# The delta rule's triangular inverse in 32x32 blocks, turned on VectorE

## What is computed

```python
decay = jnp.exp(jnp.where(causal, gc[..., :, None] - gc[..., None, :], -jnp.inf))
kb = k * beta[..., None]
lower = jnp.where(strict, jnp.einsum('nhcid,nhcjd->nhcij', kb, k) * decay, 0.0)
rhs = jnp.concatenate([v * beta[..., None], kb * jnp.exp(gc)[..., None]], axis=-1)
uw = lax.linalg.triangular_solve(lower, rhs, left_side=True, lower=True, unit_diagonal=True)
...
def step(state, inp):
    u_c, w_c, qk_c, qg_c, kd_c, a_c = inp
    v_new = u_c - jnp.einsum('nhik,nhkv->nhiv', w_c, state)
    o = jnp.einsum('nhik,nhkv->nhiv', qg_c, state) + jnp.einsum('nhij,nhjv->nhiv', qk_c, v_new)
    state = state * a_c[..., None, None] + jnp.einsum('nhjk,nhjv->nhkv', kd_c, v_new)
    return state, o
```

## Time and profile before

| | |
|---|---|
| three executions | 3165.36, 3160.8, 3163.7 us; median 3163.7 |
| the profiled execution | 3158.29 us, span 3156.2 us |
| mean granted clock of TensorE | 0.97 |
| TensorE busy | 2999.3 us, 95% of the span |
| GpSimd, ScalarE, VectorE busy | 1617.3, 1248.1, 1244.8 us |
| the chain that ended last | TensorE 85%, VectorE 5%, GpSimd 4%, ScalarE 3% |

### The profile page before, as it was taken

How to read it: one execution, slowest core, us unless ns; L and a number is a source line. 1 busy time by engine, 2 the same in 40 slices (tenths; PEclk the granted TensorE clock), 3 DMA queues, 4 the chain that set the end, 5 groups by cost and what they waited for, 6 DMA issues and landing times.

```text
span 3156.2 us, 47130 instructions
## 1 busy us (share of the span) xinstructions
PE 2999.3 (95%) x19462; PEld 2584.0 (82%) x19462; DVE 1244.8 (39%) x2298; ACT 1248.1 (40%) x2122; POOL 1617.3 (51%) x810
## 2 busy tenths in 40 slices
PE   8999999989999899999999999899999898998899
PEld 5777878779999777777777888589999698997899
DVE  2222135524444422211322114745335776622570
ACT  3222234335555332222322224454445556544453
POOL 4333443344443443344433445168887276596587
PEclk9999999999999999999999999899999899998999
DMA  6544224310000144432454323435545153354255
GB/s 251 176 167 148 94 94 156 109 47 1 1 1 1 47 168 178 161 107 94 142 178 135 105 92 88 82 115 189 185 155 176 45 169 112 108 168 140 94 188 167
DMA packets 96884, 381.45 MB, mean 121 GB/s; under 512 B 10369, under 2 KB 15649, under 8 KB 87201
## 3 DMA queue, kind: packets, MB, share of 16 engines
q1 hardware_dynamic: 87456, 311.33, 30.5%
q10 hardware_dynamic: 9216, 67.11, 6.2%
HBM read 374.21 MB, written 4.19 MB: 120 GB/s over the span
## 4 chain that ended last, share of the span: by engine, by line
PE 85%; DVE 5%; POOL 4%; ACT 3%; issue 1%; DMA 1%; SPq 0%; ACTq 0%; POOLq 0%; DVEq 0%
PE bank L220 23%; PE bank L221 22%; PE bank L222 22%; PE bank L750 5%; PE bank L293 2%; POOL weights_lo L213 2%; PE bank L1388 1%; DVE norm_work L447 1%; PE bank L769 1%; DVE norm_work L441 1%; DVE square_sums L405 1%; ACT dn_xt L1036 1%; PE bank L375 1%; ACT weights_hi L203 0%; PE bank L847 0%
## 5 line engine op out<-in xcount | busy, mean ns | idle before, releaser
L213 POOL TENSOR_TENSOR weights_lo<-weights_landing,weights_hi 128x1024 fp32r<-128x1024 f32 x554 | 1334.8, 2413 | 1192.7 <-ACT weights_hi L203 1191.7
L203 ACT ACTIVATE weights_hi<-weights_landing 128x1024 fp32r<-128x1024 f32 x554 | 586.5, 1060 | 1319.6 <-PE bank L222 1238.6
L220 PE MATMUL bank<-normed_hi,weights_lo 128*128 128x256 f32 (+1 forms) x2864 | 979.6, 342 | 39.5 <-POOL normed_lo L463 23.3
L221 PE MATMUL bank<-normed_lo,weights_hi 128*128 128x256 f32 (+1 forms) x2864 | 963.5, 336 | 0.0
L222 PE MATMUL bank<-normed_hi,weights_hi 128*128 128x256 f32 (+1 forms) x2864 | 962.3, 336 | 0.0
L220 PEld LDWEIGHTS bank<-normed_hi,weights_lo 128*128 128x128 f32 x2864 | 546.3, 191 | 133.2 <-issue 32.3
L222 PEld LDWEIGHTS bank<-normed_hi,weights_hi 128*128 128x128 f32 x2864 | 545.6, 190 | 61.5
L221 PEld LDWEIGHTS bank<-normed_lo,weights_hi 128*128 128x128 f32 x2864 | 546.5, 191 | 56.3
L221 PE MATMUL bank<-hidden_lo,weights_hi 128*128 128x512 f32 (+1 forms) x960 | 329.3, 343 | 0.0
L222 PE MATMUL bank<-hidden_hi,weights_hi 128*128 128x512 f32 (+1 forms) x960 | 329.3, 343 | 0.0
L220 PE MATMUL bank<-hidden_hi,weights_lo 128*128 128x512 f32 (+1 forms) x960 | 329.3, 343 | 0.0
(11 more groups left out here) (414 smaller groups left out, 3906.0 us busy)
## 6 DMA issues: line engine op xcount, KB each, us to landing
weights_landing<-w_up SPq DMA_DIRECT2D x176, 512.0 KB, 3.5
ada_landing<-w_ada ACTq DMA_DIRECT2D x64, 1024.0 KB, 4.9
weights_landing<-w_down SPq DMA_DIRECT2D x88, 512.0 KB, 3.5
weights_landing<-w_dn SPq DMA_DIRECT2D x33, 512.0 KB, 3.5
weights_landing<-w_mlp_up SPq DMA_DIRECT2D x32, 512.0 KB, 3.5
weights_landing<-w_mlp_down SPq DMA_DIRECT2D x32, 512.0 KB, 3.6
weights_landing<-w_gate SPq DMA_DIRECT2D x24, 512.0 KB, 4.3
weights_landing<-w_xbc SPq DMA_DIRECT2D x24, 512.0 KB, 3.5
```

The costliest lines, as they stand in the source:

```text
L203: k.nc.scalar.activation(k.WH[:, u % SLOTS, :], k.W[:, u % LANDS, :], ACT.Copy).then_inc(*k.AC.mark(("unit hi", u)))
L213: k.nc.gpsimd.tensor_tensor(k.WL[:, u % SLOTS, :], k.W[:, u % LANDS, :], k.WH[:, u % SLOTS, :].bitcast(F32), ALU.subtract).then_inc(*k.PO. ...
L220: nc.tensor.matmul(out, ll, rh, start=start, stop=False, skip_group_check=True)
L221: nc.tensor.matmul(out, lh, rl, start=False, stop=False, skip_group_check=True)
```

## The change

The blocks up to 32 are kept as such. Levels 1 to 4 no longer work on 128x128 matrices but on the four 32x32 diagonal blocks of each chunk, which lie at their own partitions: `yb` and `xb` hold [128, 4 chunks, 32]. `blocks` issues one small matmul for each chunk and block, so 16 for each direction in place of 4. The turned Y is made by VectorE's blockwise transpose (`turned`) in place of TensorE's turns and ScalarE's copies. Level 5 has 32x32 products off the diagonal (two for each chunk), and `dx`, which gives the turned second block directly. Level 6 keeps its 64x64 products, with `xt` and `p6` as operands. `at` has two buffers, so levels 5 and 6 read it unmasked. GpSimd now copies the diagonal blocks of `at` together (`ad`, four copies), makes `ym`, `y0` and four masks of 128 columns each, and later spreads `xb` and `yb` to `xt` and the wide Y (`spread`, two and four copies a direction); the wide Y is zeroed once. GpSimd also takes the product `qg` from VectorE (`queries`), in its order ahead of `spread`. `kv`, `decay` and `kq` of the next head move one slot ahead, to 1, 2 and 4, and with them `tokens`, `growth`, ScalarE's `decay` and `differences`; `products` stays in slot 5. The head's first products no longer wait for turns that stood ahead of the u products of the head before.

```diff
-LEVELS = 7
+BLK, SMALL = 32, 5
+LAST = 6
...
+def pairs(d):
+    return ((0, 1), (2, 3)) if d == 0 else ((1, 0), (3, 2))
+def blocks(k, bank, at, which, lhs, rhs, name):
+    for c in range(CHUNKS):
+        for rows, to in which:
+            mm = k.nc.tensor.matmul(bank[block(to), at + c * BLK:at + (c + 1) * BLK], lhs(rows, to, c), rhs(rows, to, c), start=True, stop=True)
+    mm.then_inc(*k.PE.mark(name))
+EACH = [(b, b) for b in range(P // BLK)]
...
+def head_p_pe(k, pe, i, s, d):
+    p = i % 2
+    pe.wait_ge(*k.DV.after("head", i, "x" if s < LAST else "y", s - 1, d))
+    if s < SMALL:
+        pe.wait_ge(*k.PO.after("head", i, "lm", s, d))
+        if s == 1 and i:
+            pe.wait_ge(*k.DV.after("head", i - 1, "y", LAST, d))
+        blocks(k, k.B[d], 0, EACH, lambda r, q, c: k.lm[d][block(r), s - 1, c, :], lambda r, q, c: k.xb[p][d][block(r), c, :], ("head", i, "p", s, d))
...
+def head_dy_pe(k, pe, i, s, d):
+    p = i % 2
+    pe.wait_ge(*k.AC.after("head", i, "ps", s, d))
+    if s < SMALL:
+        blocks(k, k.B[d], 0, EACH, lambda r, q, c: k.pb[d][block(r), c, :], lambda r, q, c: k.yb[p][d][block(r), c, :], ("head", i, "dy", s, d))
...
+KV_SLOT, DECAY_SLOT, KQ_SLOT = 1, 2, 4
...
+    def masks(i, d):
+        y, ad, p = k.yb[i % 2][d], k.ad[d], i % 2
+        pool.wait_ge(*k.DV.after("head", i, "at", d, 3))
...
+        for b in range(P // BLK):
+            if b:
+                pool.wait_ge(*k.PO.after("head", i, "ad", d, b - 1))
+            nc.gpsimd.tensor_copy(ad[block(b)], k.at_[p][d][block(b), :, block(b)]).then_inc(*k.PO.mark(("head", i, "ad", d, b)))
...
+        nc.gpsimd.tensor_tensor(y[:], ad[:], level_mask(k, d, 0), ALU.mult).then_inc(*k.PO.mark(("head", i, "ym", d)))
+        pool.wait_ge(*k.PO.after("head", i, "ym", d))
+        nc.gpsimd.tensor_tensor(y[:], ident, y[:], ALU.subtract).then_inc(*k.PO.mark(("head", i, "y0", d)))
+        for s in range(1, SMALL):
+            if i:
+                pool.wait_ge(*k.PE.after("head", i - 1, "p", s, d))
+            nc.gpsimd.tensor_tensor(k.lm[d][:, s - 1], ad[:], level_mask(k, d, s), ALU.mult).then_inc(*k.PO.mark(("head", i, "lm", s, d)))
+    def spread(i, d):
...
     for i in range(DN_HEADS):
+        for d in range(2 if i + 1 < DN_HEADS else 0):
+            queries(i + 1, d)
         for d in range(2):
+            spread(i, d)
+        for d in range(2 if i + 1 < DN_HEADS else 0):
+            masks(i + 1, d)
...
+                if s < LAST:
+                    nc.scalar.activation(flat(k.pb[d][:]), B[d][:, 0:P], ACT.Copy).then_inc(*k.AC.mark(("head", i, "ps", s, d)))
...
+    def sums(i, s, d):
+        y, dy = k.yb[i % 2][d], B[d][:, 0:P]
+        dve.wait_ge(*k.PE.after(*(("head", i, "dx", d) if s == SMALL else ("head", i, "dy", s, d))))
+        if s < SMALL:
+            nc.vector.tensor_tensor(flat(y[:]), flat(y[:]), dy, ALU.subtract).then_inc(*k.DV.mark(("head", i, "y", s, d)))
...
+    def turned(i, s, d):
+        if s:
+            dve.wait_ge(*k.DV.after("head", i, "y", s, d))
+        else:
+            dve.wait_ge(*k.PO.after("head", i, "y0", d))
...
+        nc.vector.transpose(flat(k.xb[i % 2][d][:]), flat(k.yb[i % 2][d][:])).then_inc(*k.DV.mark(("head", i, "x", s, d)))
...
             for d in range(2 if levels else 0):
+                sums(i, s, d)
+            for d in range(2 if levels and s < SMALL else 0):
+                turned(i, s, d)
...
             if after and s == 6:
                 queries(i + 1)
+                for d in range(2):
+                    turned(i + 1, 0, d)
```

More of the change, by code:

```diff
@@ L865, in heads_pe @@
     head_kq_pe(k, pe, 0)
-    for d in range(2):
-        head_first_turn_pe(k, pe, 0, d)
     for i in range(DN_HEADS + 1):
         levels, after = i < DN_HEADS, i + 1 < DN_HEADS
-        for s in range(1, LEVELS):
+        for s in range(1, LAST + 1):
             for d in range(2 if levels else 0):
[L872 to L878, removed]
+                head_p_pe(k, pe, i, s, d)
             if s == 1 and i:
@@ L885, in heads_pe @@
             for d in range(2 if levels else 0):
[L886 to L891 removed]
+                head_dy_pe(k, pe, i, s, d)
             if i and s <= CHUNKS:
@@ L896, in heads_pe @@
                 head_stat_pe(k, pe, i - 1)
-            if after and s == 2:
+            if after and s == KV_SLOT:
                 head_kv_pe(k, pe, i + 1)
-            if after and s == 3:
+            if after and s == DECAY_SLOT:
                 head_decay_pe(k, pe, i + 1)
-            if after and s == 5:
+            if after and s == KQ_SLOT:
                 head_kq_pe(k, pe, i + 1)
-            for d in range(2 if levels and s < LEVELS - 1 else 0):
-                pe.wait_ge(*k.DV.after("head", i, "y", s, d))
-                turns(k, k.B[d], lambda c: k.Y[i % 2][d][:, c, :], ("head", i, "yT", s, d))
@@ L1027, in heads_act @@
                 root(3, 4)
-            if after and s == 2:
+            if after and s == KV_SLOT:
                 tokens(i + 1)
+            if after and s in (2, 3):
+                growth(i + 1, s - 2)
             if after and s in (3, 4):
-                growth(i + 1, s - 3)
-            if after and s in (4, 5):
-                decay(i + 1, s - 4)
-            for d in range(2 if levels and s < LEVELS - 1 else 0):
-                act.wait_ge(*k.PE.after("head", i, "yT", s, d))
-                nc.scalar.activation(w4(k.XT[d]), B[d][:], ACT.Copy).then_inc(*k.AC.mark(("head", i, "x", s, d)))
-        for d in range(2 if after else 0):
-            first_x(i + 1, d)
+                decay(i + 1, s - 3)
         for d in range(2 if levels else 0):
@@ L1111, in heads_dve @@
                     ins.then_inc(*k.DV.mark(("head", i - 1, "state", s - 1, d)))
-            if after and s in (3, 4):
-                differences(i + 1, s - 3)
+            if after and s in (2, 3):
+                differences(i + 1, s - 2)
             if after and s == 5:
```

186 lines of the change are left out of this document (109 added, 77 removed).

## The result

| | before | after |
|---|---|---|
| executions | 5 | 5 |
| median, us | 3161.86 (3159.61 to 3165.36) | 3059.42 (3045.72 to 3065.1) |
| the profiled execution, its span | 3158.29, 3156.2 | 3045.72, 3043.9 |
| first u of head 0, last head's u starting at | 719.8, 1024.78 | 705.5, 920.26 |
| a head, us | 43.6 | 30.7 |

In the profiled executions the difference is 112.6 us, where I forecast 65. 104.4 of it lie in this stage. The other 8 lie mostly 900 us later, in the window attention (61.8 us after, 69.1 before), which the change doesn't touch. TensorE's granted clock over that stretch was 0.97 after and 0.90 before.

The account below looks back on a forecast made before the run. TensorE was taken to bound the stage at 43.6 us a head. Slots 9.7 + 4.6 + 4.0 + 5.0 and border 11.8 gave 35.1, saving 59.5 over seven heads plus 6 in head 0: 3099 us, range 3060 to 3165.

Parts of the forecast that it names:

- slot 1: From level 1's direction 1 products to level 2: w, o, kv and blocks on TensorE at half clock, 9.7 us.
- slot 2: From level 2's first product to level 3's: scan 3.0, p 0.3, VectorE's differences behind the decay turns 1.3, together 4.6 us.
- slot 3: From level 3's first product to level 4's: scan 3.0, p 0.3, the other differences 0.7, together 4.0 us.
- slot 4: From level 4's first product to level 5's: scan's last step to its o 2.9, kq 1.8, change 0.3, together 5.0 us.
- border: From level 5's first product (p5) to the next head's direction 1 products: GpSimd's chain sets the end, 11.8 us.
- head 0 to its u: First head, no scan beside it, from its first level's products to u: 28.5 us at half clock instead of 34.7.
- TensorE's clock: Half clock from level 5 until w and kv have filled slot 1, full in slots 2 to 4; hence 9.7 us.
- rival 3: Full clock nearly throughout: slot 1 takes 6.0 us, a head 31.4, total 3067 us; chance 0.14.
- Passes side by side: Four diagonal 32x32 blocks overlap on TensorE: 0.30 us a product, 5.5 us a head, plus 2.4 for shape changes.
- Rival 5: Border takes what the levels shed, with spreading late and queries in its way: 42.3 us a head, 3152 us; chance 0.03.
- The turn on VectorE: VectorE's blockwise transpose of Y in the levels takes 0.28 us, up to twice as much allowed.
- rival 4: Small operations dear: VectorE turns 0.57 us, GpSimd copies 0.52; 38.8 us a head, 3126 us; chance 0.10.

Follow-up runs that it names:

- the single file: Kernel after with one block's 32x32 products for all four chunks issued before the next block's: 3113.62 us, ratio 0.984 to the kernel before.

## Why the prediction was wrong

Step by step, forecast and measured, us a head: slot 1 9.7 and 5.81; slot 2 4.6 and 4.41; slot 3 4.0 and 3.80; slot 4 5.0 and 5.13; border 11.8 and 11.33; head 0 to its u 28.5 and 19.6 (705.5 - 685.93). The sum goes from 35.1 to 30.5 a head, 4.6 x 7 = 32, and head 0 gives 8: some 40 more than 65, which is the 104 of the profile.

- **The step that failed is slot 1**, priced at 9.7 us and measured at 5.81, 27 of the 40 us, and two errors are in it. The smaller is a count: kv is 8 turns of one record each, as the x8 of the turns in the earlier trace rows could have told me, not 16 passes. At half clock that is 1.6 us a head, 11 in all. (Head 7 prepares no next head and has no kv at all: its slot 1 took 4.34, those of heads 1 to 6 took 6.05 in the mean. That moves 2 us from the clock's share below to kv's.)
- **The larger error is TensorE's clock**, 2.3 us a head in slot 1 (16 in all), priced at half clock throughout. The reading of the earlier trace rows was right about the fall: the blocks and waits of levels 5 and 6 bring 0.50. It was wrong about the return, which came before slot 1 or in it. With half of u it came later; what else it hangs on is open.
- **Head 0** gives 8 us, and at most 5 of them by the clock. Its slots 1 to 4 took 3.5, 3.3, 2.4 and 4.7, against 6, 5, 3.5 and 6.5. Yet slot 1 ran at half clock from end to end, and slot 2 up to 691.9:

```profile
685.93:689.44 3.51, 3.51 (x104) 3.02 (x104) 0.99 (x4) 0.88 (x2) 3.51 (x5) 0.50 0.02 5
689.44:692.72 3.28, 3.28 (x137) 2.94 (x136) 0.99 (x4) 1.48 (x4) 0.04 (x1) 0.62 0.02 5
```

  These two slots were priced too high even for half clock; kv's count is 1.6 us of the 4.2.
- **The bottom of the range** was rival 3's sum, 3067, less 7. It had slot 1 at 6.0 for full clock, with the kv count wrong. 32 x 0.111 + 1.6 = 5.15, and measured at 1.00 it is 5.17. The 0.9 us x 7 = 6 would have put the bottom at 3054, and the result inside, without the forecast itself being any better.
- **Slots 2 to 4** came out nearly right from the wrong cause. I added up the scan's chain of 3.0 and VectorE's work. The trace shows TensorE without a gap, and all that VectorE does there is hidden, as the turns made twice show. Whoever had used my statement that TensorE is no longer the bound to add work to it would have lost 56 us.
- **Passes side by side**: 0.34 us a product where I had 0.30, with the changes of shape in it: 592 x 10.7 = 6.3 us a head, where I had 5.5 and 2.4 for changes. Right, and shown by the single file; the ada strips were the right row. This is 52 us of the gain.
- **Taking the turns off TensorE** was right in the count, 48 x 0.111 = 5.3 us a head. That block turns there would cost 56 us, some two fifths of it in pauses, was in no step.
- **The border** was right in its sum and in GpSimd as its end, with copies at 0.35 and not 0.38. That u at half clock is just as long was not seen, so a shorter GpSimd chain alone gains some 8 us, and a kept clock alone nothing. Rival 5 did not happen: spreading and qg were hidden, as said.
- **The turn on VectorE** is 0.27 to 0.31 us, as taken, and rival 4's dearer price would not have mattered.

What stays open: what ends TensorE's pauses, what sets the moment at which the granted clock comes back, and why it differs between executions in stages that the change doesn't touch.

## What to carry to other kernels

When a change takes work off the full engine, add up what is left on that engine slot by slot before saying that another is the bound. Where a clock or a wait is bought back, ask which other chain ends at the same place: the two cuts at this border gained about 0 and 8 us alone and 18 together. And price small matmuls by their number too: when many are issued in a short time, TensorE pauses for nothing that the profile shows.

## What the runs showed of the hardware

- Float32 products of 32x32 blocks on the array's diagonal, writing one PSUM bank, take 10.7 ns a pass at full clock, 0.34 us for 32 passes, and 22.5 ns a pass when neighbours share a block (the single file).
- TensorE's unexplained pauses in 249 us of the stage: 20.7 us at 28 records per us (6996), 4 at 24, none at 20.
- VectorE turns 128x128 float32 blockwise from SBUF to SBUF in 0.27 to 0.31 us. GpSimd's 128x128 product takes 0.45 us, and 0.90 while VectorE multiplies two SBUF tiles; its copy of 32x128 takes 0.29.
- After a stretch of blocks and waits the granted clock is 0.50; with 8 wide passes of u behind it slot 1 took 6.8 to 7.5 us in heads 1 to 6, with 16 5.2 to 7.1, with 32 always 5.2.
- The same window attention took 61.8 us at a granted clock of 0.97, 66 at 0.92 and 69.5 at 0.88.
